# One encoder step: the top-k limit by 33 halving steps of counting passes in place of rounds of eight maxima

## The reference, cut to what matters

```python
def dsa_attn(q, k, v, qi, ki, wi, qpos, kpos, topk, tab):
    vis = chunk_visible(qpos, kpos)                  # chunks of 64 positions
    dots = jnp.einsum('bqhd,bkd->bqhk', qi, ki) * (IDX_HEAD_DIM ** -0.5)      # 4 index heads of 64
    score = jnp.einsum('bqh,bqhk->bqk', wi * (N_IDX_HEADS ** -0.5), jax.nn.relu(dots))
    score = jnp.where(vis[None], score, NEG_INF)
    _, sel = lax.top_k(score, topk)                  # ties go to the lower key index
    ...                                              # softmax attention over the selected keys
```

## Time and profile before

| | us |
|---|---|
| median of 3 runs | 1819.62 |
| lowest and highest | 1811.26, 1824.27 |
| the profiled execution, own time | 1812.12 |
| its span | 1810.3 |
| TensorE busy (matmul) | 1643.5 (91%) |
| VectorE busy | 838.8 (46%) |
| ScalarE busy | 545.6 (30%) |
| GpSimd busy | 391.2 (22%) |
| projections, about | 68 to 403 |
| attention, about | 409 to 955 |
| feed-forward, about | 999 to 1799 |

### The profile page before, as it was taken

How to read it: one execution, slowest core, us unless ns; L and a number is a source line. 1 busy time by engine, 2 the same in 40 slices (tenths; PEclk the granted TensorE clock), 3 DMA queues, 4 the chain that set the end, 5 groups by cost and what they waited for, 6 DMA issues and landing times.

```text
span 1810.3 us, 23825 instructions
## 1 busy us (share of the span) xinstructions
PE 1643.5 (91%) x8967; PEld 1363.6 (75%) x8967; DVE 838.8 (46%) x1705; ACT 545.6 (30%) x1122; POOL 391.2 (22%) x310
## 2 busy tenths in 40 slices
PE   6698999995888788889986999999999999999996
PEld 3588889983544564555643999999999999999995
DVE  0618999907667788985436121130221211202215
ACT  1734332213333443444535211111112112111112
POOL 0521111110110010010114523132232231322314
PEclk9999999995778888898987999999999999999998
DMA  7311147637222331432215120111111111111006
GB/s 257 93 42 49 49 119 224 212 118 235 79 70 57 103 112 51 120 111 62 70 47 174 51 67 28 42 46 46 46 46 32 60 33 36 46 46 46 0 1 116
DMA packets 148567, 146.94 MB, mean 81 GB/s; under 512 B 12125, under 2 KB 129182, under 8 KB 148490
## 3 DMA queue, kind: packets, MB, share of 16 engines
q1 hardware_dynamic: 147258, 141.46, 26.0%
q0 software_dynamic: 1232, 4.46, 1.3%
HBM read 126.60 MB, written 19.29 MB: 81 GB/s over the span
## 4 chain that ended last, share of the span: by engine, by line
PE 80%; DVE 7%; issue 4%; DMA 3%; ACT 3%; POOL 2%; SPq 1%; DVEq 0%; POOLq 0%; ACTq 0%
PE S L1751 29%; PE PJ L1561 13%; PE T L1766 10%; PE PJ L1680 7%; PE PJ L1766 5%; PE PJ L1719 5%; PE S L1659 4%; PE T L1637 2%; DVE sc L1366 2%; DVE work L1269 2%; DVE top L1267 1%; PE S L1599 1%; DMA ering<-r_scratch 1%; PE S L1510 1%; DMA wraw<-in_w_in 1%
## 5 line engine op out<-in xcount | busy, mean ns | idle before, releaser
L1751 PE MATMUL S<-h2h,gh 128*128 128x352 f32 (+1 forms) x1056 | 346.7, 328 | 2.0 <-DVE top L1448 2.0
L1751 PE MATMUL S<-h2h,gl 128*128 128x352 f32 (+1 forms) x1056 | 345.9, 328 | 0.0
L1751 PE MATMUL S<-h2l,gh 128*128 128x352 f32 (+1 forms) x1056 | 345.7, 327 | 0.0
L1473 DVE TENSOR_TENSOR hv<-sg,S 128x352 f32<-128x352 f32 (+1 forms) x66 | 35.2, 533 | 496.7 <-ACT sg L1182 496.7
L1751 PEld LDWEIGHTS S<-h2h,gh 128*128 128x128 f32 x1056 | 198.8, 188 | 2.6 <-issue 2.2
L1751 PEld LDWEIGHTS S<-h2l,gh 128*128 128x128 f32 x1056 | 199.5, 189 | 0.4
L1751 PEld LDWEIGHTS S<-h2h,gl 128*128 128x128 f32 x1056 | 198.6, 188 | 0.0
L1267 DVE MAX8 top<-work 128x8 f32<-128x384 f32 (+6 forms) x202 | 176.3, 873 | 4.9
L1269 DVE MATCH_REPLACE8 work<-top,work 128x384 f32<-128x384 f32 (+6 forms) x202 | 172.9, 856 | 0.0
L1561 PE MATMUL PJ<-hTh,wh 128*128 128x352 f32 (+3 forms) x504 | 168.4, 334 | 0.0
L1561 PE MATMUL PJ<-hTl,wh 128*128 128x352 f32 (+3 forms) x504 | 166.1, 329 | 0.0
(11 more groups left out here) (166 smaller groups left out, 2520.1 us busy)
## 6 DMA issues: line engine op xcount, KB each, us to landing
graw<-in_w_gu SPq DMA_DIRECT2D x44, 512.0 KB, 4.7
ada<-in_w_ada SPq DMA_DIRECT2D x20, 1024.0 KB, 7.4
draw<-in_w_down SPq DMA_DIRECT2D x22, 512.0 KB, 3.2
wraw<-in_w_in SPq DMA_DIRECT2D x20, 512.0 KB, 5.6
q_scratch<-qst SPq DMA_DIRECT2D x8, 544.0 KB, 8.8
xin<-in_x_p SPq DMA_DIRECT2D x8, 512.0 KB, 3.6
ada_more<-in_w_ada SPq DMA_DIRECT2D x4, 1024.0 KB, 11.3
xt<-in_x_p SPq DMA_DIRECT2D x8, 512.0 KB, 4.5
```

What stands on the lines that cost most here:

```text
L1751: last = pe.matmul(S[u % 2][:, 512 * part:512 * part + n], wp[:, slot, k, 128 * part:128 * part + 128], hp[:, k, c0:c0 + n], start=(k == 0 ...
```

## The change

The index products of two tiles now stand in each of blocks 3 to 5, and those of tile 8 in block 6. Two heads, one in each half of the array's rows, are issued by turns (`dots`), and a pair stands ahead of each chunk and behind the last. The modulation products move from blocks 11 to 18 to blocks 8 to 15, and SyncE's loads of their weights with them.

The 202 rounds are gone. When all scores are there, VectorE runs `search_step` 33 times: each step counts, for all seven tiles, how many scores of a row are at least a candidate (one compare-and-add instruction for a tile, whose elementwise output goes to the byte tile `scrap`), and then moves the candidates of all tiles by small operations on 128x7 tiles, each behind a wait for the one before. Step 0 counts against zero, and turns the sign of the scores where the limit is negative; steps 2 to 9 find the exponent, steps 10 to 32 halve the interval 23 times. The result is the exact k-th largest score. Only then VectorE goes on to the gates.

In the attention, each of tiles 2 to 8 gets four more stages. At the end of slot 6 of the tile before, VectorE marks scores equal to and greater than the limit (`compare`). One slot later TensorE transposes the equal marks and ScalarE evacuates them. At the end of the tile's slots 0 and 1, TensorE ranks the equal ones by a product with a triangle of ones into PJ1 (`ranks`), and VectorE keeps those of a rank that still fits (`choose`). `gate1` now holds one group's gate at a time, and is loaded again for the last tile.

```diff
+FACTORS = [2.0 ** k for k in (126, 64, 32, 16, 8, 4, 2, 1)]
+BITS = 23
+TINY = 2.0 ** -126
+STEPS = 2 + len(FACTORS) + BITS
...
+    return [t for t in TOPK_TILES if b == 3 + (t - 2) // 2]
...
-    return [ADA_FIRST + 2 * (b - 11), ADA_FIRST + 2 * (b - 11) + 1] if 11 <= b < 19 else []
+    return [ADA_FIRST + 2 * (b - 8), ADA_FIRST + 2 * (b - 8) + 1] if 8 <= b < 16 else []
...
-P_ROUNDS = 119
...
+def tie_stage(slot, lag):
+    t, rest = divmod(slot + 2 - lag, 8)
+    return t if t in TOPK_TILES and rest == 0 else None
+def eq_groups(t):
+    return [("e", t, q) for q in range((len(key_blocks(t)) + 3) // 4)]
...
+        scrap = place("scrap", [128, WORK_N], mybir.dt.uint8, late - 4 * (2 * TOK + KEYS))
...
+            sp.wait_ge(m_scaled, NT - 1)
+            load_gate1(1)
...
+            def equals_out(t):
+                for key in eq_groups(t):
+                    q = key[2]
+                    blocks = key_blocks(t)[4 * q:4 * q + 4]
+                    bank = t_wait_full(act, key)
+                    if t > 2:
+                        act.wait_ge(rank_done, rank_count(t - 1, 1))
...
+                    act_copy(eqT[:, 4 * q:4 * q + full, 0:rows_of(t)],
+                             bank[:, 0:128 * full].rearrange("p (j r) -> p j r", r=128)[:, :, 0:rows_of(t)]
+                             ).then_inc(freed(key), 1)
...
+            def counted(least_score):
+                for i, t in enumerate(TOPK_TILES):
+                    r, n, o = rows_of(t), nkeys(t), WORK0[t]
+                    last = nc.vector.tensor_scalar(scrap[0:r, o:o + n], work[0:r, o:o + n], least_score(i), None,
+                                                   ALU.is_ge, ALU.add, accum_out=rows_at(count, i))
+                    if t != TOPK_TILES[-1]:
+                        last.then_inc(vchain, 1)
+                        chain[0] += 1
+                link(last)
+            def search_step(j):
+                if j == 0:
+                    dve.wait_ge(targets_set, 3 * len(TOPK_TILES) + 1)
+                    counted(lambda i: 0.0)
+                    link(nc.vector.tensor_tensor(good[:, :], count[:, :], target[:, 0, :], ALU.is_ge))
+                    link(nc.vector.tensor_tensor(target[:, 3, :], good[:, :], target[:, 1, :], ALU.mult))
+                    link(nc.vector.tensor_tensor(target[:, 3, :], target[:, 3, :], target[:, 2, :], ALU.add))
+                    link(nc.vector.tensor_scalar(sign[:, :], good[:, :], 2.0, -1.0, ALU.mult, ALU.add))
+                    for i, t in enumerate(TOPK_TILES):
+                        r, n, o = rows_of(t), nkeys(t), WORK0[t]
+                        link(nc.vector.tensor_scalar(work[0:r, o:o + n], work[0:r, o:o + n], rows_at(sign, i), None,
+                                                     ALU.mult))
+                elif j == 1:
+                    counted(lambda i: TINY)
+                    link(nc.vector.tensor_tensor(found[:, :], count[:, :], target[:, 3, :], ALU.is_ge))
+                    link(nc.vector.memset(least[:, :], TINY))
+                    link(nc.vector.memset(cand[:, :], TINY * FACTORS[0]))
+                elif j < 2 + len(FACTORS):
+                    by = FACTORS[j - 2]
+                    counted(lambda i: rows_at(cand, i))
+                    link(nc.vector.tensor_tensor(good[:, :], count[:, :], target[:, 3, :], ALU.is_ge))
+                    link(nc.vector.tensor_scalar(good[:, :], good[:, :], by if by > 2.0 ** 25 else by - 1.0, 1.0,
+                                                 ALU.mult, ALU.add))
+                    if j < 1 + len(FACTORS):
+                        link(nc.vector.scalar_tensor_tensor(out=cand[:, :], in0=least[:, :], scalar=FACTORS[j - 1],
+                                                            in1=good[:, :], op0=ALU.mult, op1=ALU.mult))
+                    link(nc.vector.tensor_tensor(least[:, :], least[:, :], good[:, :], ALU.mult))
+                    if j == 1 + len(FACTORS):
+                        link(nc.vector.tensor_scalar(step_[:, :], least[:, :], 0.5, None, ALU.mult))
+                        link(nc.vector.tensor_tensor(cand[:, :], least[:, :], step_[:, :], ALU.add))
                 else:
-                    link(nc.vector.match_replace(out=work[0:r, o:o + n], in_to_replace=top8[0:r, :],
-                                                 in_values=work[0:r, o:o + n], imm_value=LOW))
+                    end = j == STEPS - 1
+                    counted(lambda i: rows_at(cand, i))
+                    link(nc.vector.tensor_tensor(good[:, :], count[:, :], target[:, 3, :], ALU.is_ge))
+                    link(nc.vector.scalar_tensor_tensor(out=good[:, :], in0=good[:, :], scalar=-1.0 if end else -0.5,
+                                                        in1=step_[:, :], op0=ALU.add, op1=ALU.mult))
+                    link(nc.vector.tensor_tensor(cand[:, :], cand[:, :], good[:, :], ALU.add))
+                    if not end:
+                        link(nc.vector.tensor_scalar(step_[:, :], step_[:, :], 0.5, None, ALU.mult))
+                    else:
+                        link(nc.vector.tensor_tensor(cand[:, :], cand[:, :], found[:, :], ALU.mult))
+                        link(nc.vector.tensor_tensor(cand[:, :], cand[:, :], sign[:, :], ALU.mult))
...
-                if t > TOPK_TILES[0]:
-                    for u, _ in P_LIST[EARLY_ROUNDS * (t - 3):EARLY_ROUNDS * (t - 2)]:
-                        topk_half(u, 0)
-                        topk_half(u, 1)
-            for u, _ in P_LIST[EARLY_ROUNDS * (len(TOPK_TILES) - 1):]:
-                topk_half(u, 0)
-                topk_half(u, 1)
+            dve.wait_ge(score_acc, NH_I * len(TOPK_TILES))
+            for j in range(STEPS):
+                search_step(j)
...
+            def compare(t):
+                i, r, n, o = t - 2, rows_of(t), nkeys(t), WORK0[t]
+                x, k = work[0:r, o:o + n], keep[0:r, t % 2, 0:n]
+                if t >= 4:
+                    dve.wait_ge(qk_done, 16 * (t - 1))
+                if t > 2:
+                    dve.wait_ge(keep_ready, rank_count(t - 1, 1))
+                link(nc.vector.tensor_scalar(x, x, rows_at(sign, i), None, ALU.mult))
+                nc.vector.tensor_scalar(eq[0:r, 0:n], x, rows_at(cand, i), None, ALU.is_equal).then_inc(eq_ready, 1)
+                link(nc.vector.tensor_scalar(k, x, rows_at(cand, i), None, ALU.is_gt, ALU.add,
+                                             accum_out=rows_at(count, i)))
+                link(nc.vector.tensor_tensor(rows_at(need, i), rows_at(target[:, 0, :], i), rows_at(count, i),
+                                             ALU.subtract))
+            def choose(t, q):
+                r, n = rows_of(t), nkeys(t)
+                o, w = 512 * q, min(512, n - 512 * q)
+                dve.wait_ge(rank_done, rank_count(t, q))
+                link_read(nc.vector.scalar_tensor_tensor(
+                    out=eq[0:r, o:o + w], in0=PJ[1][0:r, 0:w], scalar=rows_at(need, t - 2), in1=eq[0:r, o:o + w],
+                    op0=ALU.is_le, op1=ALU.mult), rank_count(t, q))
+                k = keep[0:r, t % 2, o:o + w]
+                nc.vector.scalar_tensor_tensor(out=k, in0=k, scalar=-1.0, in1=eq[0:r, o:o + w], op0=ALU.add,
+                                               op1=ALU.add).then_inc(keep_ready, 1)
+            def link_read(ins, n):
+                ins.then_inc(rank_read, 1)
+                dve.wait_ge(rank_read, n)
...
-                topk_at(slot, 3)
                 t = tile_at(slot, 13)
                 if t is not None:
                     gated(t)
-                t = tile_at(slot + 2, 4)
-                if t is not None and t >= 2:
-                    r, n, o = rows_of(t), nkeys(t), WORK0[t]
-                    if t >= 4:
-                        dve.wait_ge(qk_done, 16 * (t - 1))
-                    nc.vector.tensor_scalar(keep[0:r, t % 2, 0:n], work[0:r, o:o + n], LOW / 2, NEG, ALU.is_gt,
-                                            ALU.mult).then_inc(keep_ready, 1)
+                if tie_stage(slot, 0):
+                    compare(tie_stage(slot, 0))
+                for q in range(2):
+                    t = tie_stage(slot, 2 + q)
+                    if t and 512 * q < nkeys(t):
+                        choose(t, q)
...
+            def dots(t, p):
+                r, n, k0 = rows_of(t), nkeys(t), key0(t)
+                u = NH_I * (t - 2) + 2 * p
+                if u:
+                    pe.wait_ge(relu_done, u)
+                for o in range(0, n, 512):
+                    m = min(512, n - o)
+                    for hh in range(2):
+                        part = slice(64 * hh, 64 * hh + 64)
+                        last = pe.matmul(S[hh][0:r, o:o + m], iqT[part, p, 128 * t:128 * t + r],
+                                         ikD[part, k0 + o:k0 + o + m], start=True, stop=True)
+                        if o + m == n:
+                            last.then_inc(dots_done, 1)
...
+                if b == 3:
```

(38 more changed lines are left out.)

152 lines of the change are left out of this document (77 added, 75 removed).

## The result

The changed kernel takes 1784.6 us (median, 1782.1 to 1788.0) beside 1815.4 us (1809.1 to 1824.3) of the kernel before on the same chip: ratio 0.985, 95% interval 0.9818 to 0.9882. A second measurement gave 0.9838 (0.9814 to 0.9862). The profiled executions are 1812.1 and 1788.0 us. I had forecast 1803, a fall of 16 us; the medians fell by 31. It is almost the figure of rival 4, though not by rival 4 alone.

What follows compares the result with a forecast made beforehand. Bounds: TensorE in projections, SyncE's queue in slots 0 to 7, then a busy TensorE with selection on the chain. Sum -11 + 0 + 1 - 22 + 16 = -16: 1796 profiled, 1803 median; range 1790 to 1814, with rivals 1774 to 1834.

Steps and rivals of the forecast that it cites:

- rival 4: Attention: more comes off, -38, with ties at 12, as the clock rises; -36 in all, 1784 us; chance 0.15.
- The pairs, -11: Projections: index products in pairs hide relu behind a chunk, so the last chunk ends 11 us earlier; bounds -14 to -6.
- The modulation, 0: Projections: modulation products and their loads three blocks earlier gain nothing, value 0 us; bounds -1 to +6.
- The search, +1: Ahead of slot 0: VectorE's search takes 216 us, 184 to 400, ending almost with its cover; +1 us, bounds 0 to +21.
- my upper bound of 236: Search on VectorE: 236 us if each counting instruction has 0.19 us fixed cost; 216 was taken.
- rival 2: Search counts at two columns a cycle: 133 us, over by 317, total 1802; GpSimd meetings up to 31 us, hidden; chance 0.15.
- its cover: Ahead of slot 0: other work hiding the search until SyncE reaches the gates' store at 401.4; gates expected at 402.
- the 410 that I had named as a sign of being wrong: Ahead of slot 0: the forecast is wrong if the gates come after 410 us, where 402 was expected.
- the 418: Ahead of slot 0: gates coming from 418 us on turn the forecast's sum from gain to loss.
- rival 1: Between last chunk and slot 0: search outlasts its cover, 260 us, gates at 446; +27, 1847 us; chance 0.12.
- Selection leaves the attention, -22: Attention: 83 selection rounds leave VectorE, TensorE's share reaches 91% in tiles; -22 us, bounds -8 to -40.
- Ties, +16: Attention: ranking equal scores adds TensorE products, transpositions, evacuations and VectorE operations, of which little shows; +16 us, bounds +5 to +28.

Runs made afterwards that it cites:

- e4: The kernel before with index products in pairs, modulation three blocks earlier and early rounds made together behind the last score: 1804.0 us, ratio 0.9947.
- e1: The changed kernel with 20 halving steps in the mantissa in place of 23: 1768.5 us, ratio 0.9744.
- e9: The changed kernel with early gates, step sizes halved by table, and the last three search steps in pieces, mostly inside slots 0 to 11: 1771.1 us, ratio 0.9773.
- e3: The kernel before without its 83 rounds of maxima inside the attention's slots; no ties, search or pairs: 1765.8 us, ratio 0.9752.
- e2: The changed kernel without the ranking of ties, one instruction a tile keeping scores at or over the limit: 1785.5 us, ratio 0.9834.
- e10: The changed kernel itself measured and profiled once more, nothing changed: 1784.4 us, ratio 0.9838.

## Why the prediction was right and wrong

**The pairs, -11:** right. e4 gives -10.3 at slot 0 and -10 in time. The last store went at 392.8 in e4; the forecast had the last chunk's end at 391.6.

**The modulation, 0:** right as far as it shows; the gates were never waited for by the search.

**The search, +1:** the term that failed first. Its parts were nearly right: rate 1.04 ns (measured 1.04), a pass of 5.4 us (measured 5.78), a start at 184 (187.2). Over 33 steps that is 230 us instead of 216, which lies under my upper bound of 236. 7.5 of the 14 us are the stalls behind GpSimd, 2.4 the sign products behind it, and the rest, some 5, lies in the passes (5.78 us where 5.4 and an allowance of 6 us in all stood). The failed step: the meetings with GpSimd. I had the row for them and counted up to 31 us of such meetings, but only for rival 2; in my own sum they stood at nothing. And the forecast had the search end with its cover. The cover ended about where I had put it (SyncE at the gates' store: 402.1 in e4, forecast 401.4), so nothing cushioned these small misses, and the gates came at 418 instead of 402. That is past the 410 that I had named as a sign of being wrong, and at the 418 from which, by my own reckoning, nothing would be left of the gain. Cost at slot 0: 420.0 against the 403.0 that e1 reaches, 17 us (401.6 in e9); at tile 1's start 447.8 against 433.7, 14 us. It is rival 1's mechanism, at a third of its size.

**Selection leaves the attention, -22:** the step that failed with the largest weight. e3 shows -46, beyond even my bound of -40. I divided TensorE's busy time by a share of 91%, that is, I kept busy time as it was. It isn't a constant: some 28 of the 46 us are the same products at a granted clock of 0.90 instead of 0.85. It is why the kernel is faster than forecast. Rival 4 names that, with 38. (Between tiles 1 and 6 lie four tiles, not five; the 14 us are right.)

**Ties, +16:** too large, by how much stays open. e2 gives no difference in time, 1 to 6 us from tile 1 on beside the changed kernel's two profiles and e1, and 4 to 10 us in tiles 1 to 6. Against e3, which has no ties and no search, the eight profiles with ties take 6 to 15 us more from tile 1 on. The ranks' products take 13 us by their summed durations, which overlap, and the evacuations 0.47 us each, near my prices. TensorE does all of it, and its busy time from slot 0 on is 438.0 us in the changed kernel, 429.7 in e10 and 429.8 without ties, at clocks of 0.89, 0.91 and 0.89. That the work went into TensorE's gaps is my reading; no run shows it by itself.

**The sum.** In the profiles, up to tile 1's start: -10 (pairs) and +18 (the search: 14 by e1, and 4 by which e1 itself is behind e4, unexplained), +7.5 seen. From tile 1 to the last slot: -46 (rounds), +6 (ties, from this pair of profiles) and +9, which are the 9 us that e2 loses against e3, nearly all in tiles 7 and 8, where the clock is 0.90 and 0.83 instead of 0.98 and 0.93: -31 seen. The split of these 15 us goes by the one profile of e2. Together -24, where the forecast's sum had -10 for the front and -6 for the attention, -16: an error of +17 and one of -25. So the measured time owes its distance of only 18 us from the forecast to luck: two errors of opposite sign. The other 10 us between 1803 and 1785 lie between profiled execution and median: I carried 7.5 over, and the changed kernel's median is 3.3 below its profiled execution. Why the clock falls late in one kernel and not in another, with less for TensorE to do, stays open; e10 suggests that what is lost ahead of slot 0 partly comes back (slot 0 5 us later, same end), but the two profiles of one kernel are all that I have for it.

## What to carry to other kernels

Price the removal of work beside an engine whose granted clock is below full by two rows, its idle time and its busy time at the higher clock: here the second was the larger. When a chain is forecast to end with its cover, count it as late. A row that shows two engines meeting belongs in the sum itself and not only in a rival: here some 130 small VectorE operations ran beside GpSimd's 2.4 us operation of each block. What helped was to move the last steps of the chain into slots where VectorE waits. When an instruction takes ten times its like, look first at what the other engines finish at the moment it ends. And when a change shows no effect, look where the clock went before calling the work free.
